# Column sums of squares in a two-layer decoder step: GpSimd adds four groups of channels first, TensorE sums two chunks in place of eight

## The chip, the cores and the metric

The kernel runs on one core of one Trainium2 chip. A core has TensorE (PE in the tables: matmuls into PSUM; PEld is its weight load), VectorE (DVE), ScalarE (ACT), GpSimd (POOL) and the DMA queues, the chief one issued by SyncE (SP). The engines run side by side and meet at semaphores. The metric is the device time of one execution in microseconds (us).

## The reference, cut to what matters

The program is one inference step of a two-layer decoder on 256 prompt tokens and 8 x 4 sample tokens, 288 rows in all, which share the weights. The part that the change touches is the norms:

```python
def rms_norm(x, g):
    xf = x.astype(jnp.float32)
    y = xf * lax.rsqrt(jnp.mean(xf * xf, axis=-1, keepdims=True) + NORM_EPS)
    return (y * g.astype(jnp.float32)).astype(x.dtype)

def layer_norm(x, g, b):
    xf = x.astype(jnp.float32)
    mu = jnp.mean(xf, axis=-1, keepdims=True)
    xc = xf - mu
    y = xc * lax.rsqrt(jnp.mean(xc * xc, axis=-1, keepdims=True) + NORM_EPS)
    return (y * g.astype(jnp.float32) + b.astype(jnp.float32)).astype(x.dtype)
...
    def layer(x, l, pos, mem_k, mem_v, past_k, past_v):
        x = x + 0.5 * swiglu(rms_norm(x, ffn1_norm[l]), ffn1_w1[l], ffn1_w3[l], ffn1_w2[l])
        mixed, k_new, v_new, sgu_v = token_mixing(
            rms_norm(x, mix_norm[l]), pos, mem_k, mem_v, past_k, past_v, w_in[l], sgu_ln_g[l], sgu_ln_b[l],
            sgu_w[l], sgu_b[l], w_a_out[l], w_b_out[l], w_c_out[l], w_o[l])
        x = x + mixed
        x = x + 0.5 * swiglu(rms_norm(x, ffn2_norm[l]), ffn2_w1[l], ffn2_w3[l], ffn2_w2[l])
        return x, k_new, v_new, sgu_v
```

The model width is 1024; the layer norm in `token_mixing` is over 512 channels. A final `rms_norm` follows the second layer. So one execution has seven means of squares over 1024 channels, and two layer norms that each need a mean and a mean of squares over 512 channels.

## The kernel before

Activations lie transposed: 128 channels on the partitions, the 288 tokens along the free dimension, so `x` is 128 x 8 x 288 and a sum over channels is a sum over partitions and over the eight chunks. ScalarE squares `x` two chunks at a time into `work` (`square`, L967, a 128x576 instruction, four per norm, each with one count on `sq_ready`). TensorE then multiplies each chunk by a 128x128 matrix of ones in full float32, eight matmuls accumulated in the PSUM bank `sums` (`sum_squares`, L508). Every float32 matmul appears in the trace as two passes. ScalarE takes the square root with the epsilon (`deviation`, L973, `std`), VectorE the reciprocal (L1351, `rstd`).

Every weight product is done in split precision: ScalarE copies a weight tile `wraw` to `whi` (L928), VectorE subtracts to get `wlo` (`lo`, L1301), and TensorE multiplies `whi` by the high and the low part of the activations and `wlo` by the high part (L464, L484, L546). There are four such buffers, filled in a ring by SP's queue (L1795, L1846), which waits for the `lo` of the buffer's last content.

The column sums stand in TensorE's program at these places, in order: (1) in the first feed-forward of layer one, between tile 0 and tile 1; (2) after the first tile of the memory's key and value projection; (3) in the second feed-forward of layer one; (4), (5), (6) the same three in layer two; (7) at the end, before the final norm. At (1), (3), (4) and (6) the feed-forward's first tile runs on `x` times the gain, without the norm, whose factor is multiplied in later (`sil`, L1377). The layer norm's two sums (`sum_channels`, L663: four float32 matmuls each, first of `gv`, then of the squares `lnsq`) stand in the mixing stage, which is unrolled by hand in 16 steps, in the side work (`aside`) of steps 1 and 3. That stage interleaves the projection of the normed input with transposes of cached key pages, and a later stage multiplies with cached value pages (`page`, loaded by SP at L1884, consumed at L822).

GpSimd sets the starting counts of the semaphores, loads the page table, and does nothing after.

Of the kernel before, what the change touches and what calls it, by code (L numbers as in the profile page):

```python
# [21 lines left out]
ALU = mybir.AluOpType  # L22
# [6 lines left out]
KD = D // P  # L29
SEQ, DEC_B, DEC_T = 256, 8, 4  # L30
NS = DEC_B * DEC_T
T = SEQ + NS
DEPTH = 2
# [13 lines left out]
UP = FF // W  # L47
# [66 lines left out]
@contextmanager  # L114
def repeat(eng, trips, strides):

    start = {c: c.n for c in strides}
    with eng.Fori(0, trips) as i:
        for c, s in strides.items():
            c.terms.append((i, s))  # L120
        yield i
    for k, (c, s) in enumerate(strides.items()):
        c.terms.pop()
        assert c.n - start[c] == s, f"count {k} moves by {c.n - start[c]} in a turn, not {s}"
        c.n = start[c] + trips * s
# [3 lines left out]
PAIRS = 56  # L129
RES = 48  # L130
SUMS = 5
STEPS = 51
HEADS = 12
KSTEPS = 16
GATE_STEPS = 12


W_IN_COLS = [1024, 512, 1536, 0, 2048, 2560]
# [73 lines left out]
def build(nc, A):  # L212
# [12 lines left out]
    def sem(name):  # L225
        return st.enter_context(nc.semaphore(name))
# [7 lines left out]
    work = sb("work", [P, KD, T])  # L234
# [10 lines left out]
    gv = sb("gv_T", [P, 4, T])  # L245
# [55 lines left out]
    lnsq = at("ln_square", [P, 4, T], F32, vrows_at)  # L301
# [8 lines left out]
    ones = cst[:, C_ONE:C_ONE + P]  # L310
# [6 lines left out]
    sums = st.enter_context(nc.psum_tensor("sums", [P, 512], F32))  # L317
# [11 lines left out]
    h_hi = sem("h_hi_done")  # L329
    h_ready = sem("h_ready")  # L330
    sq_ready = sem("sq_ready")
    x_ready = sem("x_ready")
    sil_ready = sem("sil_ready")
    mem_row = sem("mem_rows_squared")
# [96 lines left out]
    def _(pe):  # L431
# [70 lines left out]
        def sum_squares():  # L502

            pe.wait_ge(sum_read, nsum.at(1))
            for k in range(KD):
                if k % 2 == 0:
                    pe.wait_ge(sq_ready, nsq.next())
                mm = pe.matmul(sums[:, 0:T], ones, work[:, k, :], start=k == 0, stop=k == KD - 1)  # L508
            mm.then_inc(sum_done, 1)
            nsum.next()  # L510

# [72 lines left out]
        pe.wait_ge(ld_gain, 7 * 16)  # L584
        pe.transpose(bk("gainT")[:, 0:G_ALL], grow[:], ident[0:G_ALL, 0:G_ALL]).then_inc(filled_of("gainT"), 1)

        with repeat(pe, DEPTH, {used: PAIRS, r[0]: RES, r[1]: RES, nsum: SUMS, nsq: 12, nrm: 12, hcnt: 2 * UP,
                                soft_n: HEADS}) as L:
            def memory_turn(t):

# [68 lines left out]

            def sum_channels(src):  # L660
                pe.wait_ge(sum_read, nsum.at(1))
                for k in range(4):
                    mm = pe.matmul(sums[:, 0:T], ones, src[:, k, :], start=k == 0, stop=k == 3)  # L663
                mm.then_inc(sum_done, 1)
                nsum.next()

# [31 lines left out]

            def aside(i):
                if i == 1:  # L700
                    pe.wait_ge(evac[1], r[1].at())
                    sum_channels(gv)
                elif i == 3:
                    pe.wait_ge(xc_sq, L + 1)
                    sum_channels(lnsq)
                elif i in (4, 6):
                    pe.wait_ge(evac[(i - 4) // 2], r[(i - 4) // 2].at(-1 if i == 4 else 0))
                    rotate(L, "k", i - 4)
                    rotate(L, "k", i - 3)
                elif i == 8:  # L710
                    pe.wait_ge(vn_ready, L + 1)
                    rows("vn0", L, gv, 0)
                    rows("vn1", L, gv, 1)
                elif i == 9:
                    rows("vn2", L, gv, 2)
                elif i == 10:
                    wait(empty("rep", L))
                    wait(empty("vn1", L))
                    wait(empty("vn2", L))
                    spatial(0)  # L720
                    spatial(1)
                elif i == 11:
                    spatial(2)
                    spatial(3)
                elif i == 12:
                    rows("k0", L, qk[:, 4:8, :], 0)
                    rows("k1", L, qk[:, 4:8, :], 1)
                elif i == 13:
                    rows("k2", L, qk[:, 4:8, :], 2)
                    pe.wait_ge(evac[1], r[1].at(-1))  # L730
                    rows("v2", L, work[:, 4:8, :], 2)
                elif i == 14:
                    probs_turn(0, 0)
                    probs_turn(1, 0)
                elif i == 15:
                    rows("v0", L, work[:, 4:8, :], 0)
                    rows("v1", L, work[:, 4:8, :], 1)
                    new_probs_turn(0)
# [175 lines left out]
    def _(act):  # L914
# [124 lines left out]
        with repeat(act, DEPTH, {cur: PAIRS, r[0]: RES, r[1]: RES, nsum: SUMS, nf: 4, soft_n: HEADS,  # L1039
# [85 lines left out]
            for i in range(KSTEPS):  # L1125
                u = (i + 3) % 4
                key_copy(f"kT{i}", 0, i)
                if i == 3:
                    nsum.next()
                    act.wait_ge(sum_read, nsum.at(1))  # L1130
                    act.wait_ge(out_v, L * 32 + 16)
                    act.activation(lnsq[:], gv[:], ACT.Square, scale=SGU ** -0.5).then_inc(xc_sq, 1)
                hi(u // 2, u % 2, 4 if i > 12 and u >= 2 else 8, 1)
                key_copy(f"kT{i}", 2, i)
# [794 lines left out]
    @block.gpsimd  # L1929
    def _(pool):  # L1930

        for s_ in (*lo_done, *w_used, *evac, *emptied, k_scored, v_used, h_ready, m_lo, sum_read):
            pool.sem_inc(s_, 1)
        for s_ in (out_v, out_vn):
            pool.sem_inc(s_, 16)
        pool.dma_start(ptab[:], A["page_table"].rearrange("(o b) j -> o (b j)", o=1)).then_inc(ld_page, 16)

    st.close()

# [31 lines left out]
```

## Time and profile before

| what | us |
|---|---|
| median of 3 runs | 1699.77 (1698.89 to 1701.81) |
| profiled execution, its own time | 1696.78 |
| its span | 1695.0 |
| TensorE busy | 1647.6 (97% of the span) |
| VectorE busy | 922.4 (54%) |
| ScalarE busy | 815.4 (48%) |
| GpSimd busy | 0.8 (0%) |
| granted TensorE clock, mean | 0.991 of full speed |

The span is the profiled execution from its first to its last recorded instruction; its own time is 1.78 us longer, and the median of the runs is 2.99 us above that. Busy time of TensorE is modelled from the ends of pipelined matmuls: the time that a row of matmuls costs is the distance between starts, not the duration of one. A row of a timeline gives the start, the time to the end of the last of the instructions merged in it, the engine, the line, the operation with its tiles, the count, and in brackets the idle time before it and what ended that.

### The profile page before, as it was taken

To read this page: it belongs to the slowest core of one execution; us is meant where nothing else is said; L and a number is where in the kernel's file an instruction comes from. 1 tells how busy PE (TensorE), PEld (TensorE's weight loads), DVE (VectorE), ACT (ScalarE), POOL (GpSimd) and SP (SyncE) were. 2 spreads that over 40 slices of the span, in tenths; PEclk is the share of its full clock that TensorE was granted. 3 is DMA by queue.
4 is the path that set the end of the run, shared out by engine and by line. 5 is a ranking of instruction groups with operands and counts; after the bars stand their busy time and mean duration, and the time that the engine had idled before them with its cause. 6 is when DMAs were issued, how large, how long until landed. Compare 5 with 4: busy or idle time off the path is not lost.

```text
span 1695.0 us, 35262 instructions
## 1 busy us (share of the span) xinstructions
PE 1647.6 (97%) x13185; PEld 1555.4 (92%) x13185; DVE 922.4 (54%) x1234; ACT 815.4 (48%) x1075; POOL 0.8 (0%) x5
## 2 busy tenths in 40 slices
PE   7999999999999999999999999999999999999997
PEld 7999998998768999999999999899976889999996
DVE  4555446565545565554545554556554555555545
ACT  6766344444545444444466654444544444544433
POOL 0000000000000000000000000000000000000000
PEclk9999999999999999999999999999999999999998
DMA  7555565766776455554546546667657765455453
GB/s 224 163 171 155 162 213 179 247 222 202 249 250 230 138 186 150 160 176 158 182 132 183 153 148 194 207 220 227 222 190 241 246 216 182 140 160 174 153 174 97
DMA packets 274036, 316.89 MB, mean 187 GB/s; under 512 B 12952, under 2 KB 229232, under 8 KB 273904
## 3 DMA queue, kind: packets, MB, share of 16 engines
q1 hardware_dynamic: 271088, 309.78, 57.8%
q10 hardware_dynamic: 2784, 5.39, 1.0%
q8 instruction: 78, 1.28, 0.3%
q14 instruction: 54, 0.44, 0.1%
q0 software_dynamic: 32, 0.00, 0.0%
HBM read 309.35 MB, written 5.77 MB: 186 GB/s over the span
## 4 chain that ended last, share of the span: by engine, by line
PE 89%; DVE 5%; ACT 3%; issue 2%; DMA 1%; SPq 0%; DVEq 0%; ACTq 0%
PE res L464 44%; PE res L546 17%; PE res L484 12%; PE bank L559 6%; PE bank L648 2%; PE sums L508 1%; PE sums L822 1%; PE bank L766 1%; DVE wlo L1301 1%; ACT whi L928 1%; ACT soft L1205 1%; DVE stat L1687 1%; DVE work L1363 0%; PE bank L573 0%; PE sums L663 0%
## 5 line engine op out<-in xcount | busy, mean ns | idle before, releaser
L1301 DVE TENSOR_TENSOR wlo<-wraw,whi 128x1024 fp32r<-128x1024 f32 (+1 forms) x452 | 509.3, 1146 | 424.3 <-ACT whi L928 423.7
L928 ACT ACTIVATE whi<-wraw 128x1024 fp32r<-128x1024 f32 (+1 forms) x452 | 443.3, 994 | 287.0 <-PE res L546 143.8
L464 PE MATMUL res<-norm_hi,whi 128*128 128x288 f32 x1632 | 487.0, 298 | 14.0 <-DVE wlo L1301 11.3
L464 PE MATMUL res<-norm_lo,whi 128*128 128x288 f32 x1632 | 483.6, 296 | 0.0
L464 PE MATMUL res<-norm_hi,wlo 128*128 128x288 f32 x1632 | 482.1, 295 | 0.0
L464 PEld LDWEIGHTS res<-norm_hi,whi 128*128 128x128 f32 x1632 | 308.0, 189 | 15.3 <-issue 7.7
L464 PEld LDWEIGHTS res<-norm_hi,wlo 128*128 128x128 f32 x1632 | 309.4, 190 | 0.0
L464 PEld LDWEIGHTS res<-norm_lo,whi 128*128 128x128 f32 x1632 | 308.5, 189 | 0.2
L546 PE MATMUL res<-h_hi,whi 128*128 128x288 f32 x704 | 208.7, 296 | 0.0
L546 PE MATMUL res<-h_lo,whi 128*128 128x288 f32 x704 | 207.7, 295 | 0.0
L546 PE MATMUL res<-h_hi,wlo 128*128 128x288 f32 x704 | 207.2, 294 | 0.0
L484 PE MATMUL res<-norm_hi,whi 128*128 128x288 f32 x544 | 169.6, 312 | 0.0
L484 PE MATMUL res<-norm_lo,whi 128*128 128x288 f32 x544 | 160.1, 294 | 0.0
L484 PE MATMUL res<-norm_hi,wlo 128*128 128x288 f32 x544 | 160.1, 294 | 0.0
L546 PEld LDWEIGHTS res<-h_hi,wlo 128*128 128x128 f32 x704 | 132.5, 188 | 0.0
L546 PEld LDWEIGHTS res<-h_lo,whi 128*128 128x128 f32 x704 | 132.2, 188 | 0.0
L546 PEld LDWEIGHTS res<-h_hi,whi 128*128 128x128 f32 x704 | 132.0, 187 | 0.0
L1099 ACT ACTIVATE kT<-bank 128x512 f32<-128x512 f32 x80 | 47.8, 597 | 129.5 <-PE bank L559 129.5
L484 PEld LDWEIGHTS res<-norm_hi,whi 128*128 128x128 f32 x544 | 102.2, 188 | 7.5 <-issue 7.3
L484 PEld LDWEIGHTS res<-norm_lo,whi 128*128 128x128 f32 x544 | 102.5, 188 | 0.2
L484 PEld LDWEIGHTS res<-norm_hi,wlo 128*128 128x128 f32 x544 | 102.2, 188 | 0.0
L1509 DVE COPY kT<-bank 128x512 f32<-128x512 f32 x80 | 55.1, 689 | 78.3 <-PE bank L559 77.7
(206 smaller groups left out, 1972.7 us busy)
## 6 DMA issues: line engine op xcount, KB each, us to landing
wraw<-in_ffn_w SPq DMA_DIRECT2D x244, 512.0 KB, 4.1
wraw<-in_w_in SPq DMA_DIRECT2D x96, 512.0 KB, 4.1
page<-in_cache_k SPq DMA_DIRECT2D x128, 256.0 KB, 3.8
page<-in_cache_v SPq DMA_DIRECT2D x128, 256.0 KB, 4.1
wraw<-in_ffn_w SPq DMA_DIRECT2D x32, 384.0 KB, 3.2
wraw<-in_w_mem_kv SPq DMA_DIRECT2D x16, 512.0 KB, 3.6
page<-in_cache_mem_k SPq DMA_DIRECT2D x32, 256.0 KB, 4.5
page<-in_cache_mem_v SPq DMA_DIRECT2D x32, 256.0 KB, 5.4
```

The lines of the kernel that those rows point to most:

```text
L464: mm = pe.matmul(res[:, 2 * s + c, 0:n], w_, m_, start=h == 0 and k == 0 and i == 0, stop=h == 1 and k == kh - 1 and i == 2)
L484: mm = pe.matmul(res[:, 2 * s + c, 0:T], w_, m_, start=h == 0 and k == 0 and i == 0, stop=h == 1 and k == kh - 1 and i == 2)
L508: mm = pe.matmul(sums[:, 0:T], ones, work[:, k, :], start=k == 0, stop=k == KD - 1)
L546: mm = pe.matmul(res[:, 2 * ps + c, 0:T], w_, m_, start=part == 0 and h == 0 and k == 0 and i == 0, stop=part == 2 and h == 1 and k == kh ...
L559: mm = pe.transpose(d, i_, ident[0:i_.shape[0], 0:i_.shape[0]])
L648: mm = pe.matmul(out(bb), q_[:, c, bb, :], kTb[bb][:, c, :], start=c == 0, stop=c == 3)
L766: mm = pe.matmul(bk(nm)[:, qt * 256:(qt + 1) * 256], lhs, rhs, start=True, stop=True)
L822: mm = pe.matmul(bk(nm)[32 * bb:32 * bb + 32, :], PT[:, j, 32 * bb:32 * bb + 32], page[slot(V0 + v, bb)][:], start=j == 0, stop=j == 7)
L928: act.activation(whi[u][:, 0:kh, :], wraw[u][:, 0:kh, :], ACT.Copy).then_inc(hi_done[u], 1)
L1099: act.activation(kTb[bb][:], bk(f"{name}_{bb}")[:, :].rearrange("p (c m) -> p c m", c=4), ACT.Copy)\
L1301: dve.tensor_tensor(wlo[u][:, 0:kh, :], wraw[u][:, 0:kh, :], whi[u][:, 0:kh, :].bitcast(F32), ALU.subtract)\
L1509: dve.tensor_copy(kTb[bb][:], bk(f"{name}_{bb}")[:, :].rearrange("p (c m) -> p c m", c=4))\
```

## The change

GpSimd gets a program. For each norm it waits for the four counts of `sq_ready` in turn and adds the second, third and fourth pair of chunks onto the first pair, in place in `work`: three 128x576 float32 additions, each of which reads the one before it and so waits for its semaphore (`pool_step`). The last one counts `sq_added`, for which TensorE waits before it sums the two chunks that are left, where it waited for the four squares one by one and summed eight chunks. For the layer norm GpSimd adds the two halves of `gv` into `lnsq` and, after the square, the two halves of `lnsq` (128x576 each), and TensorE sums two chunks in place of four. The wait for an output transfer that frees `lnsq`'s memory (`out_v`) goes from ScalarE to GpSimd. The computation's result is the same up to the order of the float32 additions.

```diff
         def sum_squares():
 
             pe.wait_ge(sum_read, nsum.at(1))
-            for k in range(KD):
-                if k % 2 == 0:
-                    pe.wait_ge(sq_ready, nsq.next())
-                mm = pe.matmul(sums[:, 0:T], ones, work[:, k, :], start=k == 0, stop=k == KD - 1)
+            pe.wait_ge(sq_added, nsq.next())
+            for k in range(2):
+                mm = pe.matmul(sums[:, 0:T], ones, work[:, k, :], start=k == 0, stop=k == 1)
             mm.then_inc(sum_done, 1)
             nsum.next()
...
             def sum_channels(src):
                 pe.wait_ge(sum_read, nsum.at(1))
-                for k in range(4):
-                    mm = pe.matmul(sums[:, 0:T], ones, src[:, k, :], start=k == 0, stop=k == 3)
+                for k in range(2):
+                    mm = pe.matmul(sums[:, 0:T], ones, src[:, k, :], start=k == 0, stop=k == 1)
                 mm.then_inc(sum_done, 1)
                 nsum.next()
...
                 if i == 1:
-                    pe.wait_ge(evac[1], r[1].at())
-                    sum_channels(gv)
+                    pe.wait_ge(ch_added, L * 2 + 1)
+                    sum_channels(lnsq)
                 elif i == 3:
-                    pe.wait_ge(xc_sq, L + 1)
+                    pe.wait_ge(ch_added, L * 2 + 2)
                     sum_channels(lnsq)
...
                     act.wait_ge(sum_read, nsum.at(1))
-                    act.wait_ge(out_v, L * 32 + 16)
                     act.activation(lnsq[:], gv[:], ACT.Square, scale=SGU ** -0.5).then_inc(xc_sq, 1)
...
+        def add_squares():
+
+            for g in range(4):
+                pool.wait_ge(sq_ready, nsq.next())
+                if g:
+                    a = pool.tensor_tensor(work[:, 0:2, :], work[:, 0:2, :], work[:, 2 * g:2 * g + 2, :], ALU.add)
+                    if g < 3:
+                        a.then_inc(pool_step, 1)
+                        pool.wait_ge(pool_step, steps.next())
+                    else:
+                        a.then_inc(sq_added, 1)
+
+        add_squares()
+        with repeat(pool, DEPTH, {nsq: 12, steps: 6, r1: RES}) as L:
+            add_squares()
+            r1.n += MIX_TILES
+            pool.wait_ge(evac[1], r1.at())
+            pool.wait_ge(out_v, L * 32 + 16)
+            pool.tensor_tensor(lnsq[:, 0:2, :], gv[:, 0:2, :], gv[:, 2:4, :], ALU.add).then_inc(ch_added, 1)
+            pool.wait_ge(xc_sq, L + 1)
+            pool.tensor_tensor(lnsq[:, 0:2, :], lnsq[:, 0:2, :], lnsq[:, 2:4, :], ALU.add).then_inc(ch_added, 1)
+            r1.n += RES - MIX_TILES
+            add_squares()
+            add_squares()
```

On TensorE, at the sums of a feed-forward (place 1, and 3, 4 and 6 alike), the program before reads so, with the semaphores that an instruction waits for in brackets:

```order
L464 MATMUL res<-norm_hi,wlo_58 128x288
L504 ISA
L508 MATMUL sums<-work,consts 128x288 [waits sq_ready,sum_read]
L508 MATMUL sums<-work,consts 128x288
L508 MATMUL sums<-work,consts 128x288 [waits sq_ready]
L508 MATMUL sums<-work,consts 128x288
L508 MATMUL sums<-work,consts 128x288 [waits sq_ready]
L508 MATMUL sums<-work,consts 128x288
L508 MATMUL sums<-work,consts 128x288 [waits sq_ready]
L508 MATMUL sums<-work,consts 128x288
L464 MATMUL res<-norm_hi,whi_55 128x288 [waits lo_done2,evac1]
```

At the same place the changed program reads so (L511 is the sum, L468 the product of weights):

```order
L468 MATMUL res<-norm_hi,wlo_58 128x288
L508 ISA
L509 ISA [waits sum_read]
L511 MATMUL sums<-work,consts 128x288 [waits sq_added]
L511 MATMUL sums<-work,consts 128x288
L468 MATMUL res<-norm_hi,whi_55 128x288 [waits lo_done2,evac1]
```

Six matmuls are gone, nothing has changed places, and the one wait that is left is for GpSimd, not for ScalarE. On GpSimd the program before ends with the load of the page table:

```order
L1958 MEMSET const-bfloat16-1.0 128x1
L1958 MEMSET const-uint8-127 128x1
L1929 UNCONDITIONAL_BRANCH [waits barrier_Pool_Activation_PE_DVE_SP_gather]
L1936 DMA page_ids<-in_page_table 1x16x4
L1938 UNCONDITIONAL_BRANCH
```

In the change the body of GpSimd's loop over the layers begins so (L1947 adds squares, L1960 and L1962 the layer norm's halves):

```order
L1947 TENSOR_TENSOR work<-work 128x576 [waits sq_ready]
L1950 ISA
L1945 REGISTER_ALU [waits pool_step]
L1947 TENSOR_TENSOR work<-work 128x576 [waits sq_ready]
L1950 REGISTER_ALU
L1945 REGISTER_ALU [waits pool_step]
L1947 TENSOR_TENSOR work<-work 128x576 [waits sq_ready]
L1958 ISA
L1959 ISA [waits evac1]
L1960 TENSOR_TENSOR ln_square<-gv_T 128x576 [waits out_v]
L1961 REGISTER_ALU
L1962 TENSOR_TENSOR ln_square<-ln_square 128x576 [waits xc_squares]
```

All of it is new, and nothing else stands in GpSimd's queue in the loop.

## Rows read from the trace of the kernel before

**Rows 1.** The page's chain that ended last: share of the span by engine.

```profile
PE 89%; DVE 5%; ACT 3%; issue 2%; DMA 1%; SPq 0%; DVEq 0%; ACTq 0%
```

**Rows 2.** Groups by line on TensorE: form, count; busy us, mean ns; idle before.

```profile
L508 PE MATMUL sums<-work,consts 128*128 128x288 f32 x112 | 28.6, 407 | 0.4 <-ACT work L967 0.4
```

**Rows 3.** Timeline of TensorE at places 1, 2 and 3.

```profile
23.58 4.04 PE L508 MATMUL sums<-work,consts 128*128 128x288 f32 x16
...
239.65 4.05 PE L508 MATMUL sums<-work,consts 128*128 128x288 f32 x16
...
635.82 4.04 PE L508 MATMUL sums<-work,consts 128*128 128x288 f32 x16
```

**Rows 4.** Timeline of ScalarE: the squares ahead of places 1, 2 and 3.

```profile
17.08 0.67 ACT L967 ACTIVATE work<-x_T 128x576 f32<-128x576 f32 x1
...
18.61 0.66 ACT L967 ACTIVATE work<-x_T 128x576 f32<-128x576 f32 x1
...
20.12 0.67 ACT L967 ACTIVATE work<-x_T 128x576 f32<-128x576 f32 x1
...
235.80 0.69 ACT L967 ACTIVATE work<-x_T 128x576 f32<-128x576 f32 x1 [2.86 <-DVE x_T L1337]
...
631.39 0.67 ACT L967 ACTIVATE work<-x_T 128x576 f32<-128x576 f32 x1
```

**Rows 5.** Timeline of VectorE ahead of place 1.

```profile
17.21 1.22 DVE L1301 TENSOR_TENSOR wlo<-wraw,whi 128x1024 fp32r<-128x1024 f32 x1
18.73 1.23 DVE L1301 TENSOR_TENSOR wlo<-wraw,whi 128x1024 fp32r<-128x1024 f32 x1 [0.30 <-ACT whi L928]
20.25 1.23 DVE L1301 TENSOR_TENSOR wlo<-wraw,whi 128x1024 fp32r<-128x1024 f32 x1 [0.29 <-ACT whi L928]
```

**Rows 6.** Timeline of TensorE and ScalarE at layer one's layer norm.

```profile
299.57 0.65 ACT L955 ACTIVATE gv_T<-res 128x576 f32<-128x576 f32 x1
...
306.97 2.10 PE L663 MATMUL sums<-gv_T,consts 128*128 128x288 f32 x8
...
317.37 1.16 ACT L1132 ACTIVATE ln_square<-gv_T 128x1152 f32<-128x1152 f32 x1
...
321.07 2.10 PE L663 MATMUL sums<-ln_square,consts 128*128 128x288 f32 x8
```

**Rows 7.** Timeline of TensorE and ScalarE at place 7, the end.

```profile
1675.08 3.07 PE L508 MATMUL sums<-work,consts 128*128 128x288 f32 x12
1678.55 1.24 PE L508 MATMUL sums<-work,consts 128*128 128x288 f32 x4 [0.40 <-ACT work L967]
...
1677.83 0.67 ACT L967 ACTIVATE work<-x_T 128x576 f32<-128x576 f32 x1
...
1679.46 1.28 ACT L973 ACT_TABLE_LOAD   x1
1680.75 0.50 ACT L973 ACTIVATE std<-sums,consts 128x288 f32<-128x288 f32 x1
```

**Rows 8.** Groups by line and form on VectorE.

```profile
L1351 DVE RECIPROCAL rstd<-std 128x288 f32<-128x288 f32 x9 | 17.6, 1950 | 30.7 <-ACT std L973 30.7
...
L1337 DVE TENSOR_TENSOR x_T<-x_T,sil 128x576 f32<-128x576 f32 x16 | 12.1, 757 | 0.6
```

**Rows 9.** Who waited for whom: SP's queue and TensorE, whole span.

```profile
SPq L1846 <- DVE wlo L1301: 235.9, 78, 7.8
...
PE sums L822 <- DMA page<-in_cache_v: 6.1, 3, 2.9
```

**Rows 10.** TensorE after two stalls; two stretches with the granted clock (third number from the end).

```profile
264.33 0.40 PE L464 MATMUL res<-norm_hi,whi 128*128 128x288 f32 x1 [3.36 <-DVE wlo L1301]
...
1096.08 0.40 PE L464 MATMUL res<-norm_hi,whi 128*128 128x288 f32 x1 [3.35 <-DVE wlo L1301]
...
265.10:268.30 3.20, 3.20 (x16) 3.20 (x15) 2.58 (x3) 1.24 (x2) 0.00 (x0) 0.50 0.75 221
1097.00:1100.40 3.40, 3.40 (x28) 3.40 (x27) 2.43 (x3) 1.09 (x2) 0.00 (x0) 1.00 0.83 239
```

More of the change, by code:

```diff
@@ L135 @@
 GATE_STEPS = 12
+MIX_TILES = UP + 2 + 4
 W_IN_COLS = [1024, 512, 1536, 0, 2048, 2560]
@@ L331, in build @@
     sq_ready = sem("sq_ready")
+    sq_added = sem("sq_added")
+    ch_added = sem("channels_added")
+    pool_step = sem("pool_step")
     x_ready = sem("x_ready")
@@ L585, in _ @@
         pe.transpose(bk("gainT")[:, 0:G_ALL], grow[:], ident[0:G_ALL, 0:G_ALL]).then_inc(filled_of("gainT"), 1)
-        with repeat(pe, DEPTH, {used: PAIRS, r[0]: RES, r[1]: RES, nsum: SUMS, nsq: 12, nrm: 12, hcnt: 2 * UP,
+        with repeat(pe, DEPTH, {used: PAIRS, r[0]: RES, r[1]: RES, nsum: SUMS, nsq: 3, nrm: 12, hcnt: 2 * UP,
                                 soft_n: HEADS}) as L:
@@ L1936, in _ @@
         pool.dma_start(ptab[:], A["page_table"].rearrange("(o b) j -> o (b j)", o=1)).then_inc(ld_page, 16)
+        nsq, steps = Count(), Count()
+        r1 = Count(1)
+        def add_squares():
[20 more added lines that the diff above has]
+            add_squares()
     st.close()
```

## The prediction

> **What bounds the kernel now.** I read the chain that ended last first, since it says whose time is worth anything: 89% of the span is TensorE's own work [rows 1]. So a pass taken out of TensorE's program shortens the run by the distance between two starts, as long as what TensorE needs next has been ready for at least that time. The groups by line say how much work is at stake: the norms' sums at L508 are 112 passes, that is seven places of eight matmuls at two passes each, with 407 ns for one and almost no idle time ahead of them [rows 2]. The duration is not the price, because passes overlap. The timeline gives the price: 16 passes take 4.04 us to the end of the last [rows 3]; without the last one's 0.41 us that is 3.63 us for 15 steps, 0.242 us each. The layer norm's eight passes give the same, (2.10 - 0.41)/7 = 0.241 [rows 6].
>
> The second thing to read is how long ScalarE's last square has been done when TensorE comes to the sums, for in that gap GpSimd must now fit. At place 1 the last square ends at 20.12 + 0.67 = 20.79 and the sums start at 23.58: 2.79 us. At place 2 it is 236.49 to 239.65, 3.16 us; at place 3, 632.06 to 635.82, 3.76 us [rows 3, 4]. Layer two repeats 2 and 3 as places 5 and 6, and place 4 has more room than any. At the layer norm `gv` is whole at 300.22 for sums at 306.97, and the square ends at 318.53 for sums at 321.07: 6.75 and 2.54 us [rows 6]. Place 7 is another case: there TensorE has run out of other work, does the first 12 passes while it waits, and the last four only after the last square [rows 7].
>
> **What the change takes out.** Places 1 to 6 lose 12 passes each: 6 x 12 x 0.242 = 17.4 us. The four channel sums lose four passes each: 4 x 4 x 0.242 = 3.9 us. Together 21.3 us, if no wait takes their place. The four squares and their instructions on ScalarE stay. What follows a sum (square root, reciprocal, the scaled product) moves forward with it, as do the weight buffers that TensorE gives back, since these wait for TensorE and VectorE and for nothing that comes at a fixed time.
>
> **What it adds.** 25 GpSimd additions of 128x576, on an idle engine, and no row shows GpSimd doing arithmetic. From below the same operation and shape on VectorE bounds it, 0.757 us; from above I take the slowest elementwise rate in the trace, the reciprocal's 1.950 us for 288 elements, which makes 3.9 us for 576 [rows 8]. Below nothing it can't be. I take 1.5 us, twice the VectorE row, which is the row nearest to it in operation, shape and operands; the doubling is my allowance for a start, a semaphore's way and a slower engine. With 1.5 us one addition after the last square fits into every gap above (2.54 us is the shortest). At place 1 all three stand behind one another, but the squares come 1.5 us apart (ends 17.75, 19.27, 20.79 [rows 4]), so the last ends near 22.3, ahead of 23.58. Cost there: nothing, hidden by the first tile's matmuls; if that cover were gone, 1.5 us.
>
> The Trainium skill, "GPSIMD Engine Reference", section 3.1, measures a float32 addition on GpSimd at 1.96 times VectorE's and advises VectorE for such work. An estimate from its ratio would be 1.96 x 0.757 = 1.5 us, and the sum by it would be the same.
>
> At place 7 the addition is on the path. Before, the sums ended at 1678.55 + 1.24 = 1679.79, yet the square root began only at 1680.75, held by ScalarE's own table load (1679.46 + 1.28 = 1680.74) [rows 7]. After: the last square ends at 1678.50, the addition at 1680.0, four passes take 3 x 0.242 + 0.41 = 1.13, end 1681.13. That is 0.4 us later than now, and no gain, since the passes taken out lay in idle time.
>
> **VectorE beside GpSimd.** No row shows the two together. If an addition and a `wlo` subtraction, each with two inputs in SBUF, shut each other out for the whole instruction, place 1 goes so: `wlo` to 18.43, addition to 19.93, `wlo` (now late) to 21.16, addition to 22.66, `wlo` to 23.89, addition to 25.39, and TensorE, due at 23.58, waits 1.8 us [rows 3, 5]. At the other places a single addition after the last square meets at most one `wlo` of 1.23 us: 1.5 + 1.23 = 2.73 us fits into 3.16 and 3.76, and misses 2.54 by 0.2. VectorE's own delay of at most one addition I cost at nothing, because a `wlo` is needed only when TensorE has worked through the other three buffers; without that cover it would be up to 1.5 us for each addition that meets one. So the sum without this is 21.3 - 0.4 = 20.9 us, with it 1.8 and twice 0.2 less, 18.7 us.
>
> The Trainium skill states just this lock in "SBUF — State Buffer", section "Who interferes with whom": a VectorE instruction with two SBUF inputs and a GpSimd instruction that reads SBUF block each other, and whichever starts first holds the port. It speaks against the change, and by it the sum would be the 18.7 us.
>
> With the additions undisturbed 20.9, with the two in each other's way 18.7: I take 19.8 us in the middle. From the profiled execution's 1696.78 that is 1677.0; the median of the runs lies 2.99 us above that execution, so **1680 us**, 1.2% less.
>
> **The rivals.**
>
> *The gain is swallowed later, by page loads.* Per layer 2.9 + 2.9 + 1.9 = 7.7 us of the gain lies ahead of the stage that multiplies with cached value pages, where TensorE waits for transfers, 6.1 us in all [rows 9]. If those pages came at fixed times, 15.5 us of 21.3 would be lost: 21.3 - 15.5 - 0.4 = 5.4, 1694 us; half of it, 1687. Against it: the load queue itself waits 235.9 us for VectorE's `wlo` [rows 9], so loads are issued at TensorE's pace and move forward with it. Chance 0.14.
>
> *A slow GpSimd.* With an addition of length a, the loss is a - 1.1 at place 7, 3a - 5.8 at place 1, and twice each of a - 3.2, a - 3.8 and a - 2.5 at places 2 and 5, 3 and 6, and the second channel sums. At a = 3.9 that is 2.8 + 5.9 + 1.4 + 0.2 + 2.8 = 13.1 of 21.3, leaving 8.2: 1692 us. Chance 0.08. **The other side:** the same loss grows by 10 us per us of a, passes 21.3 at a = 4.7 and makes the kernel slower by over 0.2% (3.4 us) from a = 5.1, 6.7 times the VectorE row; at 5.5 it is 1707 us. For it speaks only that no row prices GpSimd; against it, that every elementwise row of this size is under 0.8 us but the reciprocal. Chance 0.06.
>
> *The clock.* After a stall of 3.36 us the granted clock was 0.50, the level of 1.2 GHz, for a stretch of 3.2 us, which costs 1.6 us; after the same stall in layer two it stayed at 1.00, 2.4 GHz [rows 10]. So a shift of a few us alone can add or take away such stretches; two either way are 3.2 us, which I put into the range. As a rival: TensorE waits for GpSimd at all eleven sums, and each wait is followed by such a stretch, 11 x 1.6 = 17.6 us. Then 3 us are left, 1696 us, no measurable change: the change would not do what it says. Against it: I find a wait of 1.8 us at one place, and 0.2 at two. Chance 0.06.
>
> **How the numbers follow.** The forecast has the remaining 0.66; its own range is 1675 to 1684 (gain 20.9 to 18.7, clock stretches 3.2 us either way). The others reach from 1687 over 1692 and 1694 up to 1707. The range 1676 to 1692 takes in the upper bound of the addition and half of the swallowing, and leaves out some 2 in 10: the full swallowing, the clock, the slow side and the forecast's fringe. Runs of the kernel spread over 0.17%, so 0.2% (3.4 us) is about what a measurement can tell from no change. Faster are the forecast, the swallowing and the slow GpSimd up to its bound, 0.66 + 0.14 + 0.08 = 0.88; same 0.06; slower 0.06.
>
> **What would show it.** L508's successor should have 28 passes, the channel sums 16 in all, with 0.242 us between passes. The distance from the first sum to the next weight product at places 1 to 6 should be four passes, 1.0 us, where it is 16 passes, 3.9 us, now. GpSimd should show 25 additions of 0.8 to 2 us, the last at each place done before TensorE comes; at place 7 the square root should follow the addition and not the table load. An addition over 2.5 us, a wait of TensorE on GpSimd at more places than the first, a growth of the waits for value pages by several us, or new stretches at clock 0.50 behind the sums would each make the prediction wrong by the amount worked out above.

## The result, and the profile after

The changed kernel takes 1681.42 us (median of 4 runs, 1679.5 to 1682.98), the kernel before beside it 1699.37 us (4 runs, 1698.89 to 1701.81): a ratio of 0.9891, with a 95% interval of 0.9876 to 0.9907. The forecast was 1680. The profiled execution has an own time of 1682.17 us, 14.6 us less than that of before.

The page of the changed kernel, from its head, its busy times and its chain (which answer to [rows 1]):

```profile
span 1680.4 us, 35131 instructions
...
PE 1627.9 (97%) x13085; PEld 1540.6 (92%) x13085; DVE 941.1 (56%) x1234; ACT 815.2 (49%) x1075; POOL 42.3 (3%) x30
...
PE 85%; DVE 5%; issue 5%; ACT 3%; DMA 1%; POOL 0%; ACTq 0%; SPq 0%; DVEq 0%; POOLq 0%
```

TensorE still sets the time, and its busy time fell by 19.7 us. GpSimd's additions are not on the chain, apart from the three ahead of the last norm. The sums, by tile (count, mean, the stretch in which they lie), answer to [rows 2]:

```profile
L511 PE MATMUL sums<-work,consts x28: 405/406/820, 24.8 to 1665.8; 128*128 128x288 f32 x28
L666 PE MATMUL sums<-ln_square,consts x16: 405/406/406, 302.4 to 1138.8; 128*128 128x288 f32 x16
```

28 passes stand where 112 were, and 16 channel passes where 32 were. The timeline of TensorE in the changed kernel, at places 1, 2 and 3 and between the second and the third at the first channel sum ([rows 3] and [rows 6] before):

```profile
24.51 0.29 PE L468 MATMUL res<-norm_hi,wlo 128*128 128x288 f32 x1
24.79 1.24 PE L511 MATMUL sums<-work,consts 128*128 128x288 f32 x4
25.65 0.51 PE L468 MATMUL res<-norm_hi,whi 128*128 128x288 f32 x1
...
238.08 1.14 PE L511 MATMUL sums<-work,consts 128*128 128x288 f32 x4
238.84 0.49 PE L468 MATMUL res<-mem_hi,whi 128*128 128x256 f32 x1
...
302.44 1.13 PE L666 MATMUL sums<-ln_square,consts 128*128 128x288 f32 x4
...
628.74 1.13 PE L511 MATMUL sums<-work,consts 128*128 128x288 f32 x4
629.50 0.51 PE L468 MATMUL res<-norm_hi,whi 128*128 128x288 f32 x1
```

The timeline of TensorE before, at place 1, the neighbours of the first of [rows 3]:

```profile
23.45 0.29 PE L464 MATMUL res<-norm_hi,wlo 128*128 128x288 f32 x1
...
27.24 0.51 PE L464 MATMUL res<-norm_hi,whi 128*128 128x288 f32 x1
```

At places 2 and 3 the next weight product starts 0.76 us after the first sum. Before, at place 1, that distance was 27.24 - 23.58 = 3.66: 2.90 us saved, twelve passes of 0.242. (The prediction's sign had 1.0 and 3.9 for these distances, 0.2 us too long for both; the difference, which is the gain, is the same.) At place 1 the sums now start 0.28 us after the last product instead of 0.13, and the next product 0.86 later.

A **ledger** is made from such rows, for this kernel and for each experiment: at each of the eleven sums the distance from the last weight product ahead of it to the first other matmul behind it, in the kernel before less in the kernel at hand. The changed kernel gains 2.66 at place 1, 2.91 at each of places 2 to 6, 0.97 at each of the four channel sums, and loses 1.96 at place 7. That is 2.66 + 14.55 + 3.88 - 1.96 = 19.1 us. The spans differ by 14.6 us, so 4.5 us of it are gone again outside the places, of which more below.

GpSimd's additions, by form (busy, mean ns of one, idle time before):

```profile
L1947 POOL TENSOR_TENSOR work<-work 128x576 f32<-128x576 f32 x21 | 35.8, 1704 | 1468.5 <-ACT work L970 1468.4
L1962 POOL TENSOR_TENSOR ln_square<-ln_square 128x576 f32<-128x576 f32 x2 | 2.8, 1420 | 31.7 <-ACT ln_square L1134 31.7
L1960 POOL TENSOR_TENSOR ln_square<-gv_T 128x576 f32<-128x576 f32 x2 | 2.8, 1416 | 118.8 <-ACT gv_T L958 118.8
```

An addition that meets no VectorE instruction, or starts ahead of the one that it meets, takes 1.42 to 1.44 us; those of the squares are recorded with 1.70 on average. Why, the timeline shows where GpSimd and VectorE run side by side, at place 1 and ahead of place 2. It merges instructions that follow closely, so the same start stands with one, two and three of them:

```profile
17.50 1.23 DVE L1303 TENSOR_TENSOR wlo<-wraw,whi 128x1024 fp32r<-128x1024 f32 x1
18.19 1.82 POOL L1947 TENSOR_TENSOR work<-work 128x576 f32<-128x576 f32 x1 [14.65 <-ACT work L970]
19.02 2.07 DVE L1303 TENSOR_TENSOR wlo<-wraw,whi 128x1024 fp32r<-128x1024 f32 x1 [0.29 <-ACT whi L931]
18.19 4.18 POOL L1947 TENSOR_TENSOR work<-work 128x576 f32<-128x576 f32 x2 [14.65 <-ACT work L970]
19.02 4.44 DVE L1303 TENSOR_TENSOR wlo<-wraw,whi 128x1024 fp32r<-128x1024 f32 x2 [0.29 <-ACT whi L931]
18.19 6.55 POOL L1947 TENSOR_TENSOR work<-work 128x576 f32<-128x576 f32 x3 [14.65 <-ACT work L970]
...
216.65 1.22 DVE L1303 TENSOR_TENSOR wlo<-wraw,whi 128x1024 fp32r<-128x1024 f32 x1
217.41 1.75 POOL L1947 TENSOR_TENSOR work<-work 128x576 f32<-128x576 f32 x1 [16.15 <-ACT work L970]
```

Read the ends: VectorE 18.73, GpSimd 20.01, VectorE 21.09, GpSimd 22.37, VectorE 23.46, GpSimd 24.74. The engines take turns, 1.28 us for each addition and 1.08 for each subtraction, and the recorded duration holds the wait for the other: a `wlo` that takes 1.23 us alone is recorded with 2.07. At 217.41 it is the same, an addition that ends 1.29 us after the `wlo` it met (217.87). The one that starts first is not slowed: the first `wlo` takes 1.23 us with the addition beside it from 18.19 on, and 1.22 at 216.65. So the engines don't share the time, the second waits for the first. This is what the Trainium skill, "SBUF — State Buffer", section "Who interferes with whom", says of VectorE instructions with two SBUF inputs beside GpSimd; the trace agrees, instruction by instruction.

The end of the changed kernel, with all engines ([rows 7] before):

```profile
1661.62 0.67 ACT L970 ACTIVATE work<-x_T 128x576 f32<-128x576 f32 x1
1661.86 0.95 DVE L1346 SCALAR_TENSOR_TENSOR norm_lo<-x_T,gains,norm_hi 128x288 fp32r<-128x288 f32 x2 [1.24 <-ACT norm_hi L965]
1662.37 1.70 POOL L1947 TENSOR_TENSOR work<-work 128x576 f32<-128x576 f32 x1 [15.64 <-ACT work L970]
1663.25 1.28 ACT L976 ACT_TABLE_LOAD   x1
1664.21 2.26 PE L511 MATMUL sums<-work,consts 128*128 128x288 f32 x4 [5.18 <-POOL work L1947]
1666.51 0.50 ACT L976 ACTIVATE std<-sums,consts 128x288 f32<-128x288 f32 x1 [1.97 <-PE sums L511]
```

The square root follows the last square's end (1662.29) by 4.22 us; before it was 1680.75 - 1678.50 = 2.25 [rows 7]. ScalarE's table load, which held it before, is done at 1664.53 and now waits 1.97 us for the sums.

TensorE's waits, whole span: the value pages ([rows 9] before), and the only wait for GpSimd that is recorded:

```profile
PE sums L825 <- DMA page<-in_cache_v: 5.3, 4, 2.4
PE sums L511 <- POOL work L1947: 5.2, 1, 5.2
```

Stretches of the changed kernel with the granted clock, third number from the end:

```profile
260.20:263.40 3.20, 3.20 (x15) 3.20 (x15) 2.87 (x3) 1.53 (x3) 0.00 (x0) 0.50 0.69 204
837.20:843.80 6.60, 5.31 (x22) 5.32 (x23) 2.84 (x3) 2.89 (x4) 1.71 (x1) 0.50 0.57 171
1083.00:1086.00 3.00, 3.00 (x14) 3.00 (x14) 2.56 (x3) 1.22 (x2) 0.00 (x0) 0.50 0.77 210
1664.20:1666.50 2.30, 2.26 (x4) 1.15 (x4) 0.95 (x1) 0.34 (x1) 0.00 (x0) 0.50 0.00 0
```

The first is the stretch that [rows 10] have at 265, moved forward with the program. The third lies behind the same stall as 1097 there, where the clock was 1.00; now it is 0.50, 1.2 GHz. The second is read below with the loop's turn, the fourth with the end.

### The profile page after: what moved, and what is told of

It reads as the page before. It is cut to its first block, busy times and chain, and to the rows that moved or that the text cites. A ratio compares the mean times of both kernels' runs of the same rounds, so it can differ in the third digit from the quotient of the medians.

```text
span 1680.4 us, 35131 instructions
## 1 busy us (share of the span) xinstructions
PE 1627.9 (97%) x13085; PEld 1540.6 (92%) x13085; DVE 941.1 (56%) x1234; ACT 815.2 (49%) x1075; POOL 42.3 (3%) x30
## 4 chain that ended last, share of the span: by engine, by line
PE 85%; DVE 5%; issue 5%; ACT 3%; DMA 1%; POOL 0%; ACTq 0%; SPq 0%; DVEq 0%; POOLq 0%
PE res L468 45%; PE res L549 14%; PE res L488 12%; PE bank L562 6%; PE bank L651 2%; PE sums L825 1%; PE bank L769 1%; DVE wlo L1303 1%; ACT whi L931 1%; ACT soft L1207 1%; DVE stat L1689 1%; PE sums L511 0%; DVE work L1365 0%; PE bank L576 0%; DMA page<-in_cache_v 0%
## 5 line engine op out<-in xcount | busy, mean ns | idle before, releaser
L1303 DVE TENSOR_TENSOR wlo<-wraw,whi 128x1024 fp32r<-128x1024 f32 (+1 forms) x452 | 518.5, 1167 | 410.0 <-ACT whi L931 409.4
L468 PE MATMUL res<-norm_hi,whi 128*128 128x288 f32 x1632 | 488.6, 299 | 15.9 <-DVE wlo L1303 12.0
L468 PE MATMUL res<-norm_lo,whi 128*128 128x288 f32 x1632 | 485.0, 297 | 0.0
L468 PE MATMUL res<-norm_hi,wlo 128*128 128x288 f32 x1632 | 483.3, 296 | 0.0
L468 PEld LDWEIGHTS res<-norm_hi,whi 128*128 128x128 f32 x1632 | 309.3, 189 | 17.2 <-issue 12.6
L468 PEld LDWEIGHTS res<-norm_hi,wlo 128*128 128x128 f32 x1632 | 310.8, 190 | 0.0
L468 PEld LDWEIGHTS res<-norm_lo,whi 128*128 128x128 f32 x1632 | 309.9, 190 | 0.2
```

The source lines that it names most:

```text
L468: mm = pe.matmul(res[:, 2 * s + c, 0:n], w_, m_, start=h == 0 and k == 0 and i == 0, stop=h == 1 and k == kh - 1 and i == 2)
L1303: dve.tensor_tensor(wlo[u][:, 0:kh, :], wraw[u][:, 0:kh, :], whi[u][:, 0:kh, :].bitcast(F32), ALU.subtract)\
```

## The experiments

Each stands as a difference from the changed kernel. The kernel before, beside them on the same chip, had a median of 1699.84 us for the first four and 1699.6 for the next four.

**r1: the change again**, without an edit. 

> The change as it is, run beside the three edits below on the same chip. Theory P (the passes): TensorE's program is shorter by 88 passes of 0.242 us, 21.3 us, and GpSimd's additions give back about 2 us at the end and 0.5 us at the first sums; 1679 to 1683 us, ratio to the kernel before 0.988 to 0.991. Theory S (swallowed): the same time, but because some 3 us of what the passes free are given back later at the page loads and at the places where TensorE meets the loop's start.

Measured: 1682.4 us (5 runs), ratio 0.99 (0.9885 to 0.9916). The ledger is 19.3 us, place 1 now 2.83. The profiled span is 13.7 us under that of before, so 5.6 us are given back outside the places: 2.5 of them at the loop's start, as theory S has it, 1.7 ahead of place 1 and 1.5 behind layer two's stall, but only 0.3 in the stretches that hold the page loads.

**r2: the passes alone.** The additions are left out, so the sums cover only the first two chunks; TensorE waits for the squares themselves, and GpSimd's whole program is gone:

```diff
-            pe.wait_ge(sq_added, nsq.next())
+            nsq.n += 4
+            pe.wait_ge(sq_ready, nsq.at())
...
-        add_squares()
```

> GpSimd's additions are left out, so that each norm sums only the first two of its eight chunks, and the layer norm the first two of four; TensorE waits for ScalarE's squares as before. Theory P: with nothing on GpSimd every place loses its full 2.9 us, the end keeps its start at the table load, and the time is 21 us (20 to 22.5) under the kernel before, 2 to 3 us under the change: 1677 to 1679 us. Theory S: the additions cost nothing of their own, and the time is that of the change, within 1 us: 1680 to 1682 us.

Measured: 1679.74 us (5 runs), ratio 0.988 (0.9863 to 0.9896). Its ledger is 2.91 at all of places 1 to 6, 0.97 four times, -0.18 at place 7: 21.2 us. All of GpSimd's work costs the change 2.7 us by the medians (from r1's), 1.9 to 2.0 by the ledgers, and 1.8 of that is at the end. The median lies between the two ranges expected, and the runs of r1 and r2 overlap (1681.03 to 1685.71 and 1676.05 to 1681.81), so it is the ledgers that tell theory P from S. The timeline of TensorE at its end:

```profile
1661.19 2.26 PE L512 MATMUL sums<-work,consts 128*128 128x288 f32 x4 [3.40 <-ACT work L971]
```

**r3: the additions alone.** TensorE waits for GpSimd at places 1 to 6 as in the change, but does all its passes; it sums the first two chunks over and over, and the layer norm's likewise. The end is that of before:

```diff
-            for k in range(2):
-                mm = pe.matmul(sums[:, 0:T], ones, work[:, k, :], start=k == 0, stop=k == 1)
+            for k in range(KD):
+                mm = pe.matmul(sums[:, 0:T], ones, work[:, k % 2, :], start=k == 0, stop=k == KD - 1)
...
```

> GpSimd's additions and TensorE's wait for them stay at all sums but the last, which is as before the change; TensorE multiplies eight (layer norm: four) chunks again, the first two chunks over and over, so that the sums are four (two) times too large. Theory P: without the passes' gain the time is that of the kernel before plus a wait at the first sums, 0 to 1.5 us: 1699 to 1701 us, same within 0.1%. A rival W says that the gain came from one wait in place of four and from sums that no longer stop between chunks: then this kernel too would be faster than before, by 5 us or more.

Measured: 1700.59 us (12 runs), ratio 1.0007 (0.9998 to 1.0016). The one cost that its ledger shows is a wait of TensorE at place 1; the timeline:

```profile
24.14 0.29 PE L468 MATMUL res<-norm_hi,wlo 128*128 128x288 f32 x1
24.88 4.15 PE L511 MATMUL sums<-work,consts 128*128 128x288 f32 x16 [0.44 <-POOL work L1953]
28.64 0.51 PE L468 MATMUL res<-norm_hi,whi 128*128 128x288 f32 x1
```

The next product comes 4.50 us after the last one, where before had 27.24 - 23.45 = 3.79: 0.7 us. At the other ten sums the ledger is 0.00. So the additions, locked with VectorE as they are, are hidden at places 2 to 6 and at the channel sums; and rival W, that one wait in place of four brings the gain, falls.

**r4: the end of before.** At place 7 TensorE sums eight chunks and GpSimd does nothing; all else is the change:

```diff
-        sum_squares()
+        pe.wait_ge(sum_read, nsum.at(1))
+        for k in range(KD):
+            if k % 2 == 0:
+                pe.wait_ge(sq_ready, DEPTH * 12 + k // 2 + 1)
+            mm = pe.matmul(sums[:, 0:T], ones, work[:, k, :], start=k == 0, stop=k == KD - 1)
...
-            add_squares()
+            if L < DEPTH - 1:
+                add_squares()
```

> The change, but at the last norm TensorE sums eight chunks as the squares come, as before the change, and GpSimd adds nothing there. Theory P with the end's loss as the two traces show it (from the last square to the square root 2.25 us before, 4.22 us in the change): 2.0 us (1.5 to 2.5) under the change, 1678 to 1680 us, and in its trace the square root begins at the end of the table load again. If the late end was only this execution's clock and not the addition, the gain would be half of that, 0.8 to 1.1 us.

Measured: 1681.07 us (4 runs), ratio 0.9888 (0.9872 to 0.9904). The timeline of its end:

```profile
1661.61 0.67 ACT L976 ACTIVATE work<-x_T 128x576 f32<-128x576 f32 x1
...
1662.33 1.24 PE L908 MATMUL sums<-work,consts 128*128 128x288 f32 x4 [0.40 <-ACT work L976]
1663.24 1.28 ACT L982 ACT_TABLE_LOAD   x1
...
1664.54 0.50 ACT L982 ACTIVATE std<-sums,consts 128x288 f32<-128x288 f32 x1
```

The same last square at the same time, and the square root 1.97 us earlier than in the change, at the end of the table load. The time missed the range expected (1678 to 1680): the medians of r1 and r4 lie 1.3 us apart, which their spread alone would allow. The trace shows the 2.0 us, the medians don't.

**r5: every addition twice** (the second writes where nothing is read any more; the layer norm's two likewise):

```diff
-                    a = pool.tensor_tensor(work[:, 0:2, :], work[:, 0:2, :], work[:, 2 * g:2 * g + 2, :], ALU.add)
+                    pool.tensor_tensor(work[:, 0:2, :], work[:, 0:2, :], work[:, 2 * g:2 * g + 2, :], ALU.add)\
+                        .then_inc(pool_step, 1)
+                    pool.wait_ge(pool_step, steps.next())
+                    a = pool.tensor_tensor(work[:, 2 * g:2 * g + 2, :], work[:, 2 * g:2 * g + 2, :],
+                                           work[:, 2 * g:2 * g + 2, :], ALU.add)
...
```

> The change, with each of GpSimd's 25 additions followed by a second one of the same size that adds a dead pair of chunks to itself, and the count given only after it: an addition of 2.9 us in place of 1.4. The sums are unchanged. It tells whether GpSimd and VectorE really shut each other out. With the lock a waiting wlo (1.2 us) slips in between the two: the last squares are added 4 to 5 us later at the first sums, 0.8 us late at the sums after the memory's first tile, 1.9 us late at each layer norm's second sum, and 1.5 to 2 us later at the end: 9 to 13 us over the change, 1691 to 1695 us. Without a lock (each just runs slower for a moment): 2 us at the first sums, nothing after the memory's first tile, 0.3 us at each layer norm, 1.5 us at the end: 4 us over the change, 1685 to 1687 us.

Measured: 1694.28 us (8 runs), ratio 0.9967 (0.9956 to 0.9977): 11.9 us slower than the change (r1), within the 9 to 13 expected of a lock and far from the 4 without one. GpSimd's timeline at place 1, and TensorE's waits over the whole span:

```profile
17.92 1.82 POOL L1947 TENSOR_TENSOR work<-work 128x576 f32<-128x576 f32 x1 [14.38 <-ACT work L970]
19.82 2.01 POOL L1950 TENSOR_TENSOR work<-work 128x576 f32<-128x576 f32 x1
21.91 2.27 POOL L1947 TENSOR_TENSOR work<-work 128x576 f32<-128x576 f32 x1
24.26 1.15 POOL L1950 TENSOR_TENSOR work<-work 128x576 f32<-128x576 f32 x1
25.48 1.40 POOL L1947 TENSOR_TENSOR work<-work 128x576 f32<-128x576 f32 x1
26.96 1.15 POOL L1950 TENSOR_TENSOR work<-work 128x576 f32<-128x576 f32 x1
```

```profile
PE sums L511 <- POOL work L1950: 12.2, 4, 7.3
...
PE sums L666 <- POOL ln_square L1970: 2.0, 2, 1.0
```

The first three additions meet a `wlo`, the last three don't. Its ledger is 8.2 us, 11.0 under the change's: 5.2 at place 1, 0.6 at each of places 2 and 5, 1.3 at each second channel sum, 2.1 at the end. Place by place that is near what was expected of a lock (4 to 5, 0.8, 1.9, 1.5 to 2), and not without one (2, nothing, 0.3, 1.5). So the cover that hides the additions was read rightly: a second addition is too much at the second channel sums and, by less, at places 2 and 5, and is covered at places 3, 4 and 6. Of the 5.2 at place 1, 0.9 is the clock: TensorE idles 4.3 us there, a stretch at 0.50 lies from 26.2 to 33.1, and the next product starts 1.67 us after the first sum in place of 0.76.

**r6: the layer norm's channels alone**; the squares stay with TensorE:

```diff
-            pe.wait_ge(sq_added, nsq.next())
-            for k in range(2):
-                mm = pe.matmul(sums[:, 0:T], ones, work[:, k, :], start=k == 0, stop=k == 1)
+            for k in range(KD):
+                if k % 2 == 0:
+                    pe.wait_ge(sq_ready, nsq.next())
+                mm = pe.matmul(sums[:, 0:T], ones, work[:, k, :], start=k == 0, stop=k == KD - 1)
...
```

> Only the layer norm's part of the change: the seven norms sum eight chunks as before, GpSimd adds only the halves of the layer norm's channels. Theory P: 16 passes, 3.9 us under the kernel before (3 to 4.5): 1695 to 1697 us. Theory S: these passes lie right ahead of the stage that waits for value pages, so half or more of it is swallowed there: 0 to 2 us, 1698 to 1700 us.

Measured: 1698.11 us (11 runs, 1693.05 to 1700.59), ratio 0.9987 (0.9978 to 0.9997), a gain of 1.5 us between 0.5 and 3.7. The ledger shows the full 3.88 at the four sums, but the time lies in the range of theory S, and its interval ends below 3.88: part of the gain doesn't reach the time. TensorE's waits for value pages are 6.0 us in three, as before, so it isn't there that the rest went. The mean granted clock is 0.9901 over its runs and 0.9916 over those of before beside them, which may be a part of it; the rest stays open.

**r7: one chunk, and the end of before.** r4 with GpSimd adding on until one chunk is left, so that TensorE sums one in place of two at places 1 to 6:

```diff
...
+            pool.wait_ge(sq_ready, nsq.next())
+            pool.wait_ge(sq_ready, nsq.next())
+            add(0, 2, 2)
+            pool.wait_ge(sq_ready, nsq.next())
+            add(0, 4, 2)
+            add(0, 1, 1)
+            pool.wait_ge(sq_ready, nsq.next())
+            add(0, 6, 1)
+            add(0, 7, 1, True)
...
```

(`add(a, b, n)` adds `n` chunks from `b` onto those at `a`.)

> The change with the end of before (eight chunks at the last norm), and GpSimd goes further at the other six norms: it folds its pair of chunks into one while it waits for the last square, then adds the last two chunks one by one (two additions of 128x288), and TensorE multiplies one chunk. Theory P: 12 passes less than the version with the end of before, 2.9 us, against waits of 0.3 to 1 us at the first sums and at the two after the memory's first tile, since each GpSimd instruction can stand behind a wlo: 0 to 2 us under that version, 2 to 4 us under the change, 1677 to 1680 us. If two short additions cost much more than one long (over 1.2 us each), it is no faster than the version with the end of before.

Measured: 1677.45 us (4 runs, 1676.42 to 1680.24), ratio 0.9873 (0.9858 to 0.9888): the lowest median of all variants, 3.6 to 3.8 us under r4 and r8, where 0 to 2 were expected. Its timeline at place 1:

```profile
26.04 0.75 PE L510 MATMUL sums<-work,consts 128*128 128x288 f32 x2 [1.33 <-POOL work L1949]
26.41 0.51 PE L468 MATMUL res<-norm_hi,whi 128*128 128x288 f32 x1
```

The ledger is 1.80 at place 1, 3.40 at each of places 2 to 6 (fourteen passes), 0.97 four times, nothing at the end: 22.7 us, 2.0 more than r4's 20.7. The rest does not come from the sums: the two profiled spans (1675.8 and 1680.2) differ by another 2.4 us outside the places, 2.0 at the start of layer two and 1.5 behind the last sum, less 1.0 elsewhere. So of the 3.6 only the ledger's 2.0 is shown to be r7's.

**r8: r4 again**, beside r7. 

> The version with the end of before once more, to stand beside the one-chunk version on the same chip: 1678 to 1682 us.

Measured: 1681.25 us (4 runs), ratio 0.9888 (0.9873 to 0.9904), ledger 20.6.

**r9 and r10: the kernel before, profiled twice more**, for what its own executions differ in. 

> The kernel before, unchanged, for a second profile. The place-by-place comparison shows 19.1 us gained at the sums but only 14.6 us between the two profiled spans; the profiled execution of before lies 2.6 us under the median of its runs. Theory P says that this execution had few stretches of low clock (13.7 us between 30 and 1650 us, against 17.1 in the change), so another profile of the same kernel should show the stretches and the stalls at other places, and a span of 1695 to 1700 us, with sums that take exactly as long. A rival says that the change itself brings the extra stretches: then this profile repeats 13.7 us and 1695 us.

> The same once more, since one profile can't show a spread: theory P, a span of 1695 to 1700 us and 13 to 21 us of low clock, not the same as the other look; the rival, 13.7 us again.

Measured: 1696.05 and 1698.92 us for the profiled executions (spans 1694.3 and 1697.1). Their ledgers against the first profile of before are 0.00 at every place; all that differs lies between the places, up to 2.4 us from one place to the next. The low clock between 30 and 1650 us sums to 13.7 us in both: that is the rival's figure, and theory P's, another sum in each, didn't come, though r10 has the stretches at other places. TensorE comes to the first sum at 23.18 and 24.96, against 23.58 in [rows 3].

## Why the prediction was right, and where it was not

**The passes.** 17.4 + 3.9 us were put on 72 and 16 passes at 0.242. r2 has 6 x 2.91 + 4 x 0.97 = 21.3 at places 1 to 6 and the channel sums: this term was exact, and r3, where the passes stay and nothing is gained, shows that it is the whole gain.

**The addition.** 1.5 us was taken between 0.757 and 3.9; it is 1.42 where it doesn't wait, 1.87 times VectorE's 0.757 [rows 8]. The figure of 1.96 from the Trainium skill's "GPSIMD Engine Reference", section 3.1, was within 5%. The slow GpSimd falls as a rival, and with it the slower side: at 1.70 us, the mean beside VectorE, the kernel is far from the 5.1 us from which it would lose.

**The lock.** The prediction took the middle between a sum with it (18.7) and one without it (20.9). That was a choice for want of a row, and the lock is not half there but whole: the turns at place 1 follow the predicted order, with 1.28 and 1.08 us a turn instead of 1.5 and 1.23. The last addition ends at 24.74 and not at 25.39. Of the 1.8 us of waiting forecast there, 0.25 are left, since TensorE also came later, at 24.64 (24.51 and one step of 0.13) and not at 23.58. That lateness is not the change's doing: before comes at 23.18 to 24.96. TensorE's first products stand 0.24 us apart and then 0.13, and the step comes at 21.1 in the changed kernel, at 19.1 in before (the granted clock is 0.50 up to there) and at 21.4 in r10. An arrival at 23.58 would have waited 0.9 to 1.2, since the squares, too, came 0.3 later. The five profiles with these additions (the change, r1, r3, r4, r8) lose 0.1 to 0.8 us there; that it is so little is in part luck. The 0.2 at each second channel sum didn't come, since the addition started first (1.42 us for both): the `wlo` that met it came 0.9 us later and did the waiting (1.61 us at 314.01).

**The end is the step that was mis-sized**: a loss of 0.4 was forecast, 1.96 was measured. Two things were left out of that term, and the rows of the end show both. The addition was priced at 1.5 from the square's end, but it starts while VectorE forms `norm_lo`, whose two inputs lie in SBUF, and ends 1.26 us after that, 1.78 after the square (+0.28). And the four passes were priced at 1.13 us, full speed. The first twelve passes, which TensorE used to do while it waited, are gone; it idles 5.2 us, and then finds a granted clock of 0.50, the level of 1.2 GHz: 2.26 us (+1.13). The ways from GpSimd to TensorE (0.14) and on to ScalarE (0.04) make the rest: 0.28 + 1.13 + 0.18 = 1.59, and 1.97 - 0.38 is 1.59. r1's four passes take 2.26 us as well, so it is not one execution's clock. r2 confirms the second part: without any addition its four passes take 2.26 us too, and its end still loses 0.18 us; r4's trace gives all of it back.

**The sum.** 2.66 + 14.55 + 3.88 - 1.96 is 19.1, against 19.8 taken, and inside its bounds. That it lies so close is in part luck: the end cost 1.6 us more than forecast, the lock 0.25 us where its half share in the sum was 1.1. The base agrees less well: the profiled execution of before lay 2.6 us under the median of its runs, the changed one 0.75 above, so between the medians the gain is 18.0 and between the profiles 14.6.

**Swallowed by page loads.** Not so: waits for value pages are 5.3 us where they were 6.1, and the ledger's gain stays: from the second channel sum to the next place the changed kernel is 0.6 us shorter than before in layer one and 0.9 longer in layer two; there r4, r7 and r8 are 0.5 to 1.2 shorter, and r10, the kernel before, is 1.0 longer, so no loss goes with the change. What r6 lacks of its 3.88 stays open.

**The clock behind waits.** In the changed kernel no stretch of low clock follows a sum at places 1 to 6; r5, with its wait of 4.3 us, has one at place 1. But 4.5 us of the ledger's 19.1 are given back outside the places, and 1.5 of these lie behind layer two's stall for the memory's weights, the stretch at 1083: it is one of the two stretches either way that the range allowed for. A stretch of 3.4 us costs 1.5: from place 2 to the first channel sum it is 63.5 us in before, which has one there, and 62.0 in r6 and r10, which have none. Between 30 and 1650 us the stretches at 0.50 sum to 13.7 us in before, r3, r6, r9 and r10, though not all at the same places (r3's and r10's, too, are low behind that stall of layer two); to 17.1 in the change, r1, r2 and r7, to 20.5 in r4, to 23.9 in r8, and to 27.0 in r5, 3.1 of them the end of the one at place 1. So the profiles with shorter sums at places 1 to 6 show one to four more of them (r3 and r6 ran on the same chips), and r2 shows that no addition is needed for that. The runs' own mean granted clock says it less clearly: 0.9908 and 0.9916 in the two sets of before (17 and 18 runs) and 0.9910 in r3; 0.9900 in the change, 0.9898 in r1, 0.9896 in r2, 0.9893 in r8 and 0.9863 in r5; but 0.9915 in r7, whose sums are the shortest, 0.9905 in r4, and 0.9901 in r6, whose sums at places 1 to 6 are whole. Whether shorter sums cause it, or these few executions happened so, **stays open**.

**The loop's turn.** 2.0 us of the 4.5 lie at the start of layer two. The idle time ahead of TensorE's first product there is 1.2 of it; the changed kernel, and the kernel before with its stretch of low clock behind that product:

```profile
838.49 0.60 PE L468 MATMUL res<-norm_hi,whi 128*128 128x288 f32 x1 [3.88 <-DVE norm_lo L1346]
```

```profile
847.33 0.39 PE L464 MATMUL res<-norm_hi,whi 128*128 128x288 f32 x1 [2.72 <-issue]
...
848.80:852.00 3.20, 3.20 (x15) 3.20 (x15) 1.22 (x1) 0.90 (x2) 0.00 (x0) 0.50 0.46 117
```

The rest is the clock: 3.2 us of TensorE's work at 0.50 here, 5.3 in the changed kernel's stretch at 837.2 above, and 2.1 us more at the price above are 0.9. The idle time is 1.9 to 2.8 us in the kernels about as long as before (r3, r6, r9, r10) and in r5, and 3.1 to 4.5 in r1, r2, r4, r7 and r8. r4 and r8, the same kernel, differ by 1.0 (4.15 and 3.11). The profile names `norm_lo` in some and nothing in others, but `norm_lo` doesn't end it: in before the product starts 1.05 us ahead of that instruction's end (848.38), in r1 0.75 after it (839.00 and 839.75). No run took that wait apart, so its cause stays open too. The prediction had no term for it, and none for the remaining 1 us: 1.1 of later start and 0.9 ahead of place 6, both of which before has as well in r10, less 0.6 ahead of place 3 and 0.4 behind the last sum.

## What to carry to other kernels

Where TensorE sets the time, a pass that is taken from its program is worth the distance between two starts, and the work that replaced it on an idle engine was free wherever it fitted into the gap between its input's end and TensorE's arrival; measure that gap at each place, with VectorE's turn added in where it works beside GpSimd on SBUF. At a place where TensorE idles anyway, such as ahead of the last norm, passes cost nothing, and without them it came to the rest at 1.2 GHz, so leave the work there: of the variants run, the one that does so and adds down to one chunk elsewhere had the lowest median. A profile's difference of a few us between two single executions says nothing until the kernel before has been profiled more than once; a ledger at the places that the change touches does.

## What the hardware showed that was not expected

- GpSimd and VectorE, both reading SBUF, didn't both get slower: they took strict turns, 1.28 us for a GpSimd addition of 128x576 and 1.08 for a VectorE subtraction of 128x1024, and the record of the one that waited includes its wait (2.07 and 2.44 us for a `wlo` of 1.23). VectorE's mean for `wlo` still rose only from 1146 to 1167 ns, since the 25 additions held up few of the 452 subtractions (14 of 128x1024 are recorded with more than 1.3 us).
- In such a turn each instruction took less than alone: 1.28 against 1.42 us, 1.08 against 1.23. Its start is already behind it when its turn comes, as it seems; no run took that apart.
- On GpSimd an addition of a tile to itself took 1.15 us in r5, one of two different tiles 1.40.
- Behind 5.2 us of TensorE's idle time, 3.4 in r2, four passes took 2.26 us at a granted clock of 0.50 in place of 1.13, right at the chain's end; in before and r4, where twelve passes lay in that time, the last four took 1.24.
